# One block per turn in the experts' loop: single row buffers, halved evacuation of the transposed rows, and a VectorE copy of the gathered rows

## What is computed

```
u = x * (1.0 + scale2) + shift2
y_moe = _hier_moe(u, ...)            # top-1 of 4 groups, top-2 of its 8 experts
x = _layer_norm(DEEPNORM_ALPHA * x + gate2 * y_moe, ln_g[1], ln_b[1])

# _grouped_experts: the 2 x 2112 (token, expert) pairs are sorted by expert and cut in blocks of 128
def expert_block(args):
    xblk, ex = args                                              # (128, 1024), expert
    h = jax.nn.silu(xblk @ w_gate[ex]) * (xblk @ w_up[ex])       # (128, 256)
    return h @ w_down[ex]                                        # (128, 1024)
```

## Time and profile before

| | us |
|---|---|
| median of 3 runs | 1866.45 (1858.99 to 1866.88) |
| the profiled execution | 1868.97 |
| its span in the trace | 1867.3 |
| mean granted TensorE clock | 0.96 of full speed |
| PE busy | 1714.5 (92%) |
| DVE busy | 1134.7 (61%) |
| ACT busy | 621.7 (33%) |
| POOL busy | 592.1 (32%) |

### The profile page before, as it was taken

How to read it: one execution, slowest core, us unless ns; L and a number is a source line. 1 busy time by engine, 2 the same in 40 slices (tenths; PEclk the granted TensorE clock), 3 DMA queues, 4 the chain that set the end, 5 groups by cost and what they waited for, 6 DMA issues and landing times. The chain is left out here.

```text
span 1867.3 us, 28890 instructions
## 1 busy us (share of the span) xinstructions
PE 1714.5 (92%) x8860; PEld 1329.4 (71%) x8861; DVE 1134.7 (61%) x1809; ACT 621.7 (33%) x784; POOL 592.1 (32%) x705
## 2 busy tenths in 40 slices
PE   5999999999999999999698999538999999999875
PEld 2777787777888899999577878426767677677532
DVE  4667666666767676667366877844456433346358
ACT  2333323333333322222131111014556443456334
POOL 0122221122222221122025466633344333334247
PEclk8899999999999999999899999759999999999988
DMA  7443344334333323332285444159999957579986
GB/s 257 163 137 107 115 148 136 124 132 137 102 97 90 91 63 92 99 102 70 70 251 184 135 133 134 63 165 321 341 338 378 375 197 242 170 273 361 354 336 237
DMA packets 171080, 341.68 MB, mean 183 GB/s; under 512 B 18836, under 2 KB 109748, under 8 KB 165983
## 3 DMA queue, kind: packets, MB, share of 16 engines
q1 hardware_dynamic: 148518, 285.35, 45.8%
q0 software_dynamic: 17648, 54.82, 7.9%
q10 hardware_dynamic: 4818, 0.26, 0.2%
HBM read 275.81 MB, written 64.58 MB: 182 GB/s over the span
## 5 line engine op out<-in xcount | busy, mean ns | idle before, releaser
L1532 DVE TENSOR_TENSOR w_gu_lo<-w_gu_raw,w_gu_hi (+1 forms) x64 | 146.5, 2292 | 144.6 <-ACT w_gu_hi L1525 134.2
L860 DVE TENSOR_TENSOR w_lo<-w_raw,w_hi 128x1024 fp32r<-128x1024 f32 x112 | 138.6, 1241 | 132.3 <-ACT w_hi L539 129.6
L651 POOL TENSOR_TENSOR o_r<-o_ms,neg_half 128x4 f32<-128x4 f32 (+1 forms) x16 | 16.8, 1052 | 634.6 <-DVEq L914 634.6
L685 PE MATMUL pr<-ua_hi,w_hi 128*128 128x512 f32 x448 | 185.0, 413 | 9.9 <-DVE ua_lo L865 9.9
L1961 PE MATMUL py<-w_dn_w,hhT 128*128 x400 | 183.7, 603 | 8.3 <-ACT hhT L1785 4.4
L685 PE MATMUL pr<-ub_hi,w_hi 128*128 128x288 f32 (+1 forms) x672 | 189.2, 336 | 0.0
L685 PE MATMUL pr<-ub_lo,w_hi 128*128 128x288 f32 (+1 forms) x672 | 183.8, 327 | 0.0
L685 PE MATMUL pr<-ub_hi,w_lo 128*128 128x288 f32 (+1 forms) x672 | 183.6, 327 | 0.0
L1929 PE MATMUL ph<-w_gu_hi,x_hi 128*128 (+1 forms) x400 | 180.1, 450 | 2.5 <-DVE x_lo L1825 2.5
L685 PE MATMUL pr<-ua_lo,w_hi 128*128 128x512 f32 x448 | 179.1, 400 | 0.0
L685 PE MATMUL pr<-ua_hi,w_lo 128*128 128x512 f32 x448 | 179.1, 400 | 0.0
(11 more groups left out here) (334 smaller groups left out, 3388.5 us busy)
## 6 DMA issues: line engine op xcount, KB each, us to landing
w_raw<-in_w_in SPq DMA_DIRECT2D x112, 512.0 KB, 4.1
w_gu_raw<-in_w_e_gate SPq DMA_DIRECT2D x32, 1024.0 KB
w_gu_raw<-in_w_e_up SPq DMA_DIRECT2D x32, 1024.0 KB
w_dn_w<-in_w_e_down SPq DMA_DIRECT2D x32, 1024.0 KB
w_mod<-in_w_mod_rest SPq DMA_DIRECT2D x16, 1024.0 KB
y_t<-y_scratch SPq DMA_DIRECT2D x16, 1024.0 KB, 8.6
w_ring<-in_w_mod_first SPq DMA_DIRECT2D x4, 2048.0 KB, 16.5
x_cols<-in_x_prompt_t SPq DMA_DIRECT2D x32, 256.0 KB, 4.8
```

The costliest lines, as they stand in the source:

```text
L651: pool.tensor_tensor(o_r[:, 0:c], o_ms[:, 0:c], keep["neg_half"][:, 0:c], ALU.pow).then_inc(o_rs, 1)
L685: last = pe.matmul(pr[n % 2][:, a * 512:a * 512 + c], w[:, n % WS, k, :], x[:, k, a * c:(a + 1) * c], start=(k == 0 and m == 0), stop=(k = ...
L860: dve.tensor_tensor(w_lo[:, n % WS], w_raw[:, n % WRAW], w_hi[:, n % WS].bitcast(F32), ALU.subtract).then_inc(lo_done, 1)
L1532: dve.tensor_tensor(w_slot(keep["gu_lo"], s, lo, hi), w_slot(keep["gu_raw"], r, lo, hi), w_slot(keep["gu_hi"], s, lo, hi).bitcast(F32), AL ...
```

## The change

- `xg`, `x_hi`, `x_lo`, `y_sb` and `ids_cur` have one buffer each in place of two halves. A new tile `xs` holds a copy of the gathered rows: VectorE copies `xg` to `xs` (`take_rows`), TensorE transposes from `xs`.
- The transposed rows are evacuated in two halves of 512 columns. Half 0 goes as before, half 1 behind `gsig` on ScalarE and behind `gate` on VectorE.
- VectorE's turn for block g is now `x_lo(g+2)` half 0, `gate(g+1)`, `x_lo(g+2)` half 1, `take_rows(g+3)`.
- A gather waits for `xs_rdy`, the end of the copy of the block before it, in place of `xT_ps`.
- `store_rows(g)` waits for the landing of the scatter before it ahead of the copy of `ids_cur`, in place of behind `y_rdy`.
- The loops take one block per turn, and the rounding up to an even number of blocks is gone: 49 blocks run.

```diff
-        xg = sb("xg", [P, 2, D])
-        x_hi = sb("x_hi", [P, 2, KT * P], F32R)
-        x_lo = sb("x_lo", [P, 2, KT * P], F32R)
+        xg = sb("xg", [P, D])
+        xs = sb("xs", [P, D])
+        x_hi = sb("x_hi", [P, KT * P], F32R)
+        x_lo = sb("x_lo", [P, KT * P], F32R)
...
-        y_sb = sb("y_sb", [P, 2, D])
+        y_sb = sb("y_sb", [P, D])
...
-        ids_cur = sb("ids_cur", [P, 2, 4], I32)
+        ids_cur = sb("ids_cur", [P, 4], I32)
...
+        HK = KT * P // 2
...
-                def prefetch(g, half):
+                def prefetch(g):
                     ahead = g + AHEAD
                     wait_apart(pool, ids_in, 16 * ahead + 16, tick)
                     fetch_ids(ahead + 1, (ahead + 1) % RING)
                     wait_apart(pool, xg_in, 16 * ahead, tick)
-                    wait_apart(pool, xT_ps, ahead - 1, tick)
-                    gather(ahead, ahead % RING, half)
+                    wait_apart(pool, xs_rdy, ahead, tick)
+                    gather(ahead, ahead % RING)
 
-                def store_rows(g, half):
-                    pool.tensor_copy(ids_cur[:, half, :], place(ids_ring, g % RING)).then_inc(cur, 1)
+                def store_rows(g):
+                    if not (isinstance(g, int) and g == 0):
+                        wait_apart(pool, y_out, 16 * g, tick)
+                    pool.tensor_copy(ids_cur[:, :], place(ids_ring, g % RING)).then_inc(cur, 1)
                     wait_apart(pool, cur, g + 1, tick)
                     wait_apart(pool, y_rdy, g + 2, tick)
-                    if not (isinstance(g, int) and g == 0):
-                        wait_apart(pool, y_out, 16 * g, tick)
...
-                block(0, 0)
-                block(1, 1)
-                with pool.Fori(2, lead, 2) as g:
-                    block(g, 0)
-                    block(pool.snap(g + 1), 1)
-                store_rows(lead, 0)
-                store_rows(pool.snap(lead + 1), 1)
+                block(0)
+                with pool.Fori(1, lead) as g:
+                    block(g)
+                store_rows(lead)
...
-                def x_evac(b, half):
+                def x_evac(b, a):
                     act.wait_ge(xT_ps, b + 1)
...
+                    act.activation(x_hi[:, a * HK:(a + 1) * HK], px[:, a * HK:(a + 1) * HK], ACT.Copy).then_inc(x_h, 1)
...
-                        x_evac(g + 2, now)
+                        x_evac(g + 2, 0)
                         sigmoid(g + 1, nxt)
+                        x_evac(g + 2, 1)
...
+                def take_rows(b):
+                    dve.wait_ge(xg_in, 16 * b + 16)
+                    if not (isinstance(b, int) and b == 0):
+                        dve.wait_ge(xT_ps, b)
+                    dve.tensor_copy(xs[:, :], xg[:, :]).then_inc(xs_rdy, 1)
...
-                        x_evac(g + 2, dve.snap(g % 2))
+                        x_evac(g + 2, 0)
                         gate(g + 1, dve.snap((g + 1) % 2))
+                        x_evac(g + 2, 1)
+                        take_rows(g + 3)
...
-                dve.tensor_tensor(exp_tab[:, NE:NE + 1], exp_tab[:, NE:NE + 1], odd[:, :], ALU.add)
-                dve.tensor_tensor(exp_tab[:, NE + 1:NE + 2], exp_tab[:, NE + 1:NE + 2], odd[:, :], ALU.add)
...
                 for a in range(2):
                     split_low(dve, keep, 0, a, 0, 0)
+                take_rows(0)
                 x_evac(0, 0)
+                x_evac(0, 1)
+                take_rows(1)
+                x_evac(1, 0)
+                gate(0, 0)
                 x_evac(1, 1)
-                gate(0, 0)
+                take_rows(2)
...
-                def transposes(b, half):
-                    pe.wait_ge(xg_in, 16 * b + 16)
+                def transposes(b):
+                    pe.wait_ge(xs_rdy, b + 1)
                     if not (isinstance(b, int) and b == 0):
-                        pe.wait_ge(x_l, b)
+                        pe.wait_ge(x_l, 2 * b)
...
-                    pe.wait_ge(x_l, b + 1)
+                    pe.wait_ge(x_l, 2 * b + 1)
                     for k in range(KT):
                         if k == KT // 2:
                             mid()
                             pe.wait_ge(gu_l, 2 * e + 2)
+                            pe.wait_ge(x_l, 2 * b + 2)
...
-                with pe.Fori(0, lead, 2) as g:
-                    block_step(g, 0)
-                    block_step(pe.snap(g + 1), 1)
-                block_step(lead, 0)
-                last_step(pe.snap(lead + 1))
+                with pe.Fori(0, lead) as g:
+                    block_step(g)
+                last_step(lead)
```

More of the change, by code:

```diff
@@ L1599, in expert_phase @@
         eg, gst = sb("eg", [P, 1]), sb("gst", [P, 1])
-        odd = sb("odd", [1, 1], I32)
         tab_f = sb("tab_f", [P, 2])
@@ L1690, in _ @@
                 lead = blocks_before(sp, NE + 1)
-                wait_apart(sp, y_out, 16 * lead + 32, tick)
+                wait_apart(sp, y_out, 16 * lead + 16, tick)
                 wait_apart(sp, ids_in, 16 * lead + 16 * (AHEAD + 1), tick)
@@ L1703, in fetch_ids, with gather @@
                     pool.dma_start(place(ids_ring, at_ring), scr["list"][bass.ds(at * P, P), :]).then_inc(ids_in, 16)
-                def gather(b, at_ring, half):
+                def gather(b, at_ring):
                     pool.tensor_copy(ids_now[:, :], place(ids_ring, at_ring)).then_inc(kept, 1)
                     wait_apart(pool, kept, b, tick)
-                    pool.indirect_dma_start(xg[:, half, :], None, scr["u2"],
+                    pool.indirect_dma_start(xg[:, :], None, scr["u2"],
                                             bass.IndirectOffsetOnAxis(ap=ids_now[:, 0:1], axis=0)).then_inc(xg_in, 16)
@@ L1725, in _, with block @@
                     pool.wait_ge(xg_in, 16 * b)
[L1726 to L1732, removed]
-                def prefetch(g, half):
+                    pool.wait_ge(xs_rdy, b)
+                    gather(b, b)
+                def block(g):
+                    prefetch(g)
+                    store_rows(g)
+                def prefetch(g):
                     ahead = g + AHEAD
@@ L1781, in block_work @@
                 def block_work(g, gu_next, final=False):
-                    now, nxt = act.snap(g % 2), act.snap((g + 1) % 2)
+                    nxt = act.snap((g + 1) % 2)
                     if not final:
@@ L1791, in block_work @@
                     act.wait_ge(cur, g + 1)
-                    act.activation(y_sb[:, bass.ds(now, 1), :].rearrange("p a d -> p (a d)"), py[:, :], ACT.Copy,
-                                   scale=ids_cur[:, bass.ds(now, 1), 2:3].rearrange("p a c -> p (a c)").bitcast(F32)).then_inc(y_rdy, 1)
+                    act.activation(y_sb[:, :], py[:, :], ACT.Copy,
+                                   scale=ids_cur[:, 2:3].bitcast(F32)).then_inc(y_rdy, 1)
                 group_shares(act, R, *BATCH[0], gs_rdy)
@@ L1821, in split_gu, with x_evac @@
                     split_low(dve, keep, e, a, dve.snap(e % 2), dve.snap(e % RAW))
[L1823 to L1826, removed]
+                def x_evac(b, a):
+                    dve.wait_ge(x_h, 2 * b + a + 1)
+                    dve.tensor_tensor(x_lo[:, a * HK:(a + 1) * HK], px[:, a * HK:(a + 1) * HK],
+                                      x_hi[:, a * HK:(a + 1) * HK].bitcast(F32), ALU.subtract).then_inc(x_l, 1)
+                def take_rows(b):
[3 more added lines that the diff above has]
+                    dve.tensor_copy(xs[:, :], xg[:, :]).then_inc(xs_rdy, 1)
                 def gate(b, half):
@@ L1911, in expert_of @@
                     return pe.value_load(blk_tab[0:1, bass.ds(b, 1)], min_val=0, max_val=NE - 1)
[L1913 to L1914 removed]
+                def transposes(b):
+                    pe.wait_ge(xs_rdy, b + 1)
                     if not (isinstance(b, int) and b == 0):
[L1916 removed]
+                        pe.wait_ge(x_l, 2 * b)
                     for k in range(KT):
[L1918 removed]
+                        last = pe.transpose(px[:, k * P:(k + 1) * P], xs[:, k * P:(k + 1) * P], ident[:, :])
                     last.then_inc(xT_ps, 1)
@@ L1927, in gate_up @@
                             pe.wait_ge(gu_l, 2 * e + 2)
+                            pe.wait_ge(x_l, 2 * b + 2)
                         for m, (x, w) in enumerate(((x_hi, gu_hi), (x_hi, gu_lo), (x_lo, gu_hi))):
-                            last = pe.matmul(ph[:, half, :], x[:, half, k * P:(k + 1) * P], w_slot(w, s, k * GU, (k + 1) * GU),
+                            last = pe.matmul(bank(half, 0, GU), x[:, k * P:(k + 1) * P], w_slot(w, s, k * GU, (k + 1) * GU),
                                              start=(k == 0 and m == 0), stop=(k == KT - 1 and m == 2))
@@ L1942, in _ @@
                 pe.sem_inc(dn, 1)
-                transposes(0, 0)
-                gate_up(0, 0, 0, 0, lambda: transposes(1, 1))
+                transposes(0)
+                gate_up(0, 0, 0, 0, lambda: transposes(1))
                 pe.wait_ge(tab_sb, 1)
```

(8 more changed lines are left out.)

17 lines of the change are left out of this document (8 added, 9 removed).

## The result

| | before | after |
|---|---|---|
| median | 1866.28 us of 4 runs (1858.99 to 1866.88) | 1948.61 us of 4 runs (1945.72 to 1950.34) |
| the profiled execution, its span | 1868.97, 1867.3 | 1950.34, 1948.6 |
| mean granted TensorE clock | 0.96 | 0.95 |
| first load of the last stage (`y_t`) starts at | 1778.02 | 1858.97 |

The ratio is 1.0448 (95% interval 1.0428 to 1.0468): 82 us slower, where the forecast was 1955 us. The last stage begins 81 us later, so the loss lies in the experts' stage and before its end.

What follows compares the result with a forecast made beforehand. TensorE set the pace at 10.01 us a block; now a three-engine chain of waits would. From 1280.2, 557.6 us for 46 blocks give 1837.8, stage end 1866.0, +88, total 1957; predicted 1955, range 1900 to 1990.

Steps and rivals of the forecast that it cites:

- middle blocks: Experts' stage, blocks without splits behind a block without splits: gather with landing of 7.3 decides, 9.1 us each, 6 blocks.
- blocks alone with their expert: Experts' stage, one-block experts behind another expert's last block, both weight splits: 13.8 us in place of 10.01, 19 blocks.
- first blocks: First blocks of experts 2, 3, 5, 16 to 22: held-up ids_now, then gather landing of 7.3; 11.1 us each, 10 blocks.
- last blocks: Last blocks of experts with several: no split follows the copy before, ids_now through in 0.3; 11.8 us each, 11 blocks.
- T: Start of the experts' stage: end of VectorE's copy of block 3, forecast at 1280.2 us.
- The ring: Experts' stage: one-turn chain of waits through GpSimd, ScalarE and VectorE, copy to next copy; 13.8 us between one-block experts.
- recorded lower bound: Gather landing in the experts' stage: 3.3, from the lone scatter, said to give 6 to 9 us less a block.
- Padding: End of the experts' stage: 49 blocks in place of 50, ending 5 to 10 us earlier at TensorE's pace.
- Rival 1: GpSimd slips in ahead of VectorE's split: 11.8 us in single blocks, 49 less, 1906 us; chance 0.12.
- Rival 2: Experts' stage: chain of waits closes within TensorE's 10.01 us, only the padding block goes, 1859 us; chance 0.06.
- Rival 3: Experts' stage: waits in every block hold TensorE at 1.2 GHz, 118 us more, 2073 us; chance 0.04.
- rival 4: VectorE's copy 1.22: 26 us more, 1981; gather landings of 9.7: another 20; upper part of forecast's range, no own chance.

## Why the prediction was right

The mechanism was the one forecast, with one exception among the steps (the middle blocks), and the time was 6 us below the forecast. By its steps, measured as distances between the starts of the copies to `xs`, from that of block 3 to the last one of a turn with splits (1274.43 to 1828.92, 46 blocks):

| step | forecast | measured |
|---|---|---|
| copy, 128x1024 | 0.65 | 0.68 |
| 19 blocks alone with their expert | 13.8 | 13.77 |
| 10 first blocks | 11.1 | 11.9 |
| 6 middle blocks | 9.1 | 8.8 |
| 11 last blocks | 11.8 | 11.0 |
| sum of the 46 | 557.6 | 554.5 |
| end of the stage behind T | 585.8 | 583.9 |
| T, end of the copy of block 3 | 1280.2 | 1275.1 |

*The ring* held link by link: `ids_now` until 2.24 behind the copy (2.25 forecast), `y_sb` 0.10 behind `ids_cur` (0.12), 1.02 ahead of the split (1.04), then 2.21, 0.60, 0.59, 0.34, 0.60 on VectorE.

*Last blocks* were the mis-sized term, 9 us too much. I charged ScalarE's gap of 1.04 between `y_sb` and the split in every turn. It is there (1.01 to 1.07) in all 19 turns of a block that is alone with its expert; in all 11 turns of the last block of an expert with several the split follows `y_sb` without a gap:

```profile
1614.77 1.11 ACT L1792 ACTIVATE y_sb<-py,ids_cur 128x1024 f32<-128x1024 f32 x1 [4.49 <-POOL ids_cur L1747]
1615.78 1.90 ACT L1525 ACTIVATE w_gu_hi<-w_gu_raw  x1
```

The row of before from which I took the gap was put down to a DMA, and it stands in a stretch of single blocks. The trace of before shows the same two cases, so this could have been read there.

*First blocks* were too cheap by 8 us in all. The form of the sum held (`ids_now` held up, then the gather's landing), the landing did not: 7.3 was taken, and the copy came 7.5 to 9.3 behind the gather's start, 8.2 on the mean. GpSimd's gather and VectorE's copy behind it:

```profile
1626.12 0.98 POOL L1711 DMA_INDIRECT xg<-u_scratch,ids_now  x1 [0.79 <-POOL ids_now L1709]
```

```profile
1635.02 0.69 DVE L1834 COPY xs<-xg 128x1024 f32<-128x1024 f32 x1 [2.72 <-DMA xg<-u_scratch,ids_now]
```

"The slower pace asks less of the queues" was a guess, and it failed here: from this gather's start to its landing, 1626.12 to 1635.00, the DMA share was 0.95.

*Middle blocks* came out near the 9.1 by luck. I had the gather decide, with its landing at 7.3. The gathers of these six blocks landed 4.2 to 4.4 behind their start, and no copy waited for one. An example, gather and copy:

```profile
1541.09 0.99 POOL L1711 DMA_INDIRECT xg<-u_scratch,ids_now  x1 [0.79 <-DMA y_scratch<-y_sb,ids_cur]
```

```profile
1548.88 0.68 DVE L1827 TENSOR_TENSOR x_lo<-pxe,x_hi 128x512 fp32r<-128x512 f32 x1
1549.48 0.68 DVE L1834 COPY xs<-xg 128x1024 f32<-128x1024 f32 x1
```

The copy stands behind VectorE's work for the block, and that waited for TensorE's products. In the two experts of four blocks the copies came 7.34 and 7.54 apart in the first such turn and 10.35 and 10.27 in the second, while TensorE's `py` products started 10.0 to 10.6 apart: TensorE set the pace here, and the copies only caught up with it. The recorded lower bound is not right either: a landing of 3.3 in place of 7.3 takes 4.0 off a block, not 6 to 9.

The errors of the first and the last blocks nearly cancel, so the sum is better than its terms.

*Start.* Of the 5.1 us by which T was early, 3.7 are earlier stages: the first gather of the stage started at 1236.38 against 1240.12 before, with the same code ahead of it. This is within the spread of the runs (the eleven traces have it between 1235.71 and 1240.12) and no effect of the change.

*Padding.* "5 to 10 us" against 7.1 measured.

*Rivals.* Rival 1 (GpSimd slips in ahead of the split, 11.8 in the single blocks) is out: `ids_now` was 1.95 long in the rows above, starting 0.29 behind the copy's end, well inside the split. Rival 2 would need a ring of 10; it took 13.76. Rival 3 needed a granted clock near 0.5 over long stretches; it was 0.93 and the slow products cost nothing. Of rival 4, the copy was not dearer (0.68), and a landing later than 7.3 cost time only where a copy waited for it: in the first blocks, and at the start and the end of the stage.

*The port.* In the eleven traces 270 of GpSimd's small copies (`ids_now` or `ids_cur`) started inside a low split, and every one of them ended 0.04 to 0.17 us behind the split's end; the kernel in which VectorE's copy stood behind the split had short ones. The rule of the Trainium skill ("SBUF — State Buffer", section "🔬 SBUF: two separate sides"), that whoever starts first keeps the shared port pair for its whole instruction, agrees with all of them. I had put the hold-up at 2.0 us a single block; moving the split out of the way while paying for its 2.21 left 0.43, so it was worth 1.8. No run took the hold-up away without moving the work, so this number rests on a difference.

## What to carry to other kernels

When a buffer goes from two to one, follow everything that is queued behind the new wait on the waiting engine, from engine to engine, until it comes back: here a 0.68 us copy in idle time made a ring of 13.8 us round a block of 10.0. Add up that ring from rows of the trace and compare it with the block of the engine that sets the pace; only the part above it costs. A cut ring uncovers the next one (here the gather's, then the landing of the scatter), so count them all before expecting the whole gain back.

## What the runs showed of the hardware that I had not expected

- The time from the start of a gather or scatter of 128 rows of 4 KB to its landing came in two groups in the changed kernel. Of its 49 scatters 31 took 6.4 to 9.1 us, and the DMA share in that time was 0.81 or more; 18 took 3.3 to 4.2, at a share of 0.66 or less. The six gathers of the middle blocks, beside few loads of weights, took 4.2 to 4.4 at a share of 0.39 to 0.53. This is read from the traces alone, no run varied it, and two other gathers landed within 4.4 at shares of 0.84 and 0.85.
- Not only copies are held up. In the kernel with two `xg` a gather's issue, 0.98 long elsewhere, took 2.67 in one turn and 2.44 in the turn before. It ends 0.86 us behind the split inside which it started; so did, within 0.85 to 1.01 us, all 121 gathers and scatters of the eleven traces that were issued inside a low split, the one of 2.23 in the earlier trace rows among them:

```profile
1472.94 2.67 POOL L1711 DMA_INDIRECT xg<-u_scratch,ids_now  x1 [0.79 <-POOL ids_now L1709]
```

```profile
1472.46 2.29 DVE L1532 TENSOR_TENSOR w_gu_lo<-w_gu_raw,w_gu_hi  x1 [4.57 <-ACT w_gu_hi L1525]
```

- Versions in which ScalarE picks `y_sb` and `ids_cur` by a register started `y_sb` later behind its releaser (0.32 us in one, 0.22 in another, against 0.10). On a ring this is paid in every turn: 13.99 against 13.77 us in the first of them. The cause was not isolated.
